# Columns in the first memory piece, held weight transfers and a new order of ScalarE's opening in a two-stack hybrid kernel on one Trainium2 core

## The reference

```python
h = rms_norm(x, norm_pre)
proj = h @ w_in
...
mkv = rms_norm(mem, mem_norm) @ w_mem_kv
mem_k, mem_v = jnp.split(mkv, 2, axis=-1)
y_xa = flat(memory_attention(heads(xa_q), heads(mem_k), heads(mem_v)))
...
up = jnp.einsum('bsnw,nwd->bsnd', ys, w_up)
merged = jnp.sum(jax.nn.sigmoid(gates.reshape(b_, s_, N_BRANCH, D_MODEL)) * up, axis=2)
out = merged @ w_out
return x + rms_norm(out, norm_post)
```

## Time and profile before

| what | before |
|---|---|
| median of 3 runs | 1752.31 us (1752.08 to 1752.43) |
| the profiled execution | 1751.61 us, span 1749.8 us |
| TensorE busy | 1734.2 us, 99% of the span, 9136 matmuls |
| VectorE busy | 1307.9 us, 75% |
| ScalarE busy | 1017.4 us, 58% |
| GpSimd busy | 99.6 us, 6% |
| mean granted TensorE clock | 0.997 of full |
| data moved | 308.70 MB, mean 176 GB/s |
| chain that ended last | TensorE 93%, VectorE 3%, ScalarE 2% |

### The profile page before, as it was taken

How to read it: one execution, slowest core, us unless ns; L and a number is a source line. 1 busy time by engine, 2 the same in 40 slices (tenths; PEclk the granted TensorE clock), 3 DMA queues, 4 the chain that set the end, 5 groups by cost and what they waited for, 6 DMA issues and landing times.

```text
span 1749.8 us, 24255 instructions
## 1 busy us (share of the span) xinstructions
PE 1734.2 (99%) x9136; PEld 1495.1 (85%) x9136; DVE 1307.9 (75%) x1747; ACT 1017.4 (58%) x1406; POOL 99.6 (6%) x154
## 2 busy tenths in 40 slices
PE   8999999999999999999999999999999999999998
PEld 7888888888888888888889988888888988888887
DVE  6787767665877786756669787688778987678775
ACT  5676656454666755644555765755556656555544
POOL 1000000000000000000000000500003360000000
PEclk9999999999999999999999999999999999999999
DMA  9755655566765565565666554456555515356563
GB/s 303 205 156 175 181 159 166 165 187 190 248 183 161 172 181 170 156 181 169 192 194 198 182 192 157 144 182 192 191 186 188 170 37 181 121 168 189 188 189 108
DMA packets 211028, 308.70 MB, mean 176 GB/s; under 512 B 11808, under 2 KB 114848, under 8 KB 210656
## 3 DMA queue, kind: packets, MB, share of 16 engines
q1 hardware_dynamic: 208640, 299.44, 55.5%
q0 software_dynamic: 2128, 7.66, 1.3%
q10 hardware_dynamic: 144, 0.05, 0.0%
HBM read 306.06 MB, written 1.05 MB: 176 GB/s over the span
## 4 chain that ended last, share of the span: by engine, by line
PE 93%; DVE 3%; ACT 2%; issue 1%; DMA 0%; SPq 0%; DVEq 0%; ACTq 0%
PE bank L1701 51%; PE bank L1766 26%; PE bank L1733 3%; PE bank L2168 3%; PE bank L2217 2%; DVE weights_lo L1050 1%; PE bank L1816 1%; PE bank L1830 1%; PE bank L2089 1%; PE bank L2107 1%; PE bank L1799 1%; ACT weights_hi L570 1%; PE bank L1838 0%; DVE arena L1104 0%; DMA weights_raw<-in_w_mem_kv_dram 0%
## 5 line engine op out<-in xcount | busy, mean ns | idle before, releaser
L1050 DVE TENSOR_TENSOR weights_lo<-weights_raw,weights_hi 128x1024 fp32r<-128x1024 f32 x560 | 668.3, 1232 | 222.4 <-ACT weights_hi L570 216.7
L570 ACT ACTIVATE weights_hi<-weights_raw 128x1024 fp32r<-128x1024 f32 x559 | 574.4, 1056 | 395.6 <-DMA weights_raw<-in_w_in_dram 188.0
L1701 PE MATMUL bank<-weights_hi,h_parts 128*128 128x512 f32 x1856 | 567.5, 391 | 0.3 <-DVE h_parts L1482 0.2
L1701 PEld LDWEIGHTS bank<-weights_hi,h_parts 128*128 128x128 f32 x1856 | 348.0, 188 | 73.3 <-DVE h_parts L1482 0.6
L1701 PE MATMUL bank<-weights_lo,h_parts 128*128 128x512 f32 x928 | 347.5, 389 | 0.0
L1766 PE MATMUL bank<-h_parts,weights_hi 128*128 128x512 f32 (+1 forms) x1248 | 302.7, 384 | 0.9 <-DVE arena L1104 0.8
L1701 PE MATMUL bank<-weights_hi,arena_parts 128*128 128x512 f32 x928 | 269.9, 390 | 0.0
L1766 PEld LDWEIGHTS bank<-h_parts,weights_hi 128*128 128x128 f32 x1248 | 219.8, 189 | 40.5 <-DVE arena L1104 1.5
L1701 PEld LDWEIGHTS bank<-weights_lo,h_parts 128*128 128x128 f32 x928 | 174.3, 188 | 35.4
L1701 PEld LDWEIGHTS bank<-weights_hi,arena_parts 128*128 128x128 f32 x928 | 173.6, 188 | 35.4 <-ACT arena L590 0.2
L1766 PEld LDWEIGHTS bank<-h_parts,weights_lo 128*128 128x128 f32 x1248 | 169.4, 190 | 11.1
(11 more groups left out here) (306 smaller groups left out, 1629.4 us busy)
## 6 DMA issues: line engine op xcount, KB each, us to landing
weights_raw<-in_w_in_dram SPq DMA_DIRECT2D x224, 512.0 KB, 3.7
weights_raw<-in_f_w_up_dram SPq DMA_DIRECT2D x96, 512.0 KB, 3.5
weights_raw<-in_f_w_down_dram SPq DMA_DIRECT2D x48, 512.0 KB, 3.6
weights_raw<-in_w_up_dram SPq DMA_DIRECT2D x40, 512.0 KB, 3.6
weights_raw<-in_c_w_pw_dram SPq DMA_DIRECT2D x24, 512.0 KB, 3.6
weights_raw<-in_ab_w_in_dram SPq DMA_DIRECT2D x20, 512.0 KB, 3.7
weights_raw<-in_w_out_dram SPq DMA_DIRECT2D x16, 512.0 KB, 3.8
weights_raw<-in_xa_wk_dram SPq DMA_DIRECT2D x16, 512.0 KB, 3.4
```

The costliest lines, as they stand in the source:

```text
L570: nc.scalar.activation(w_hi[:, q % SPLIT, 0:w], raw[:, n % RAW, 0:w], ACT.Copy).then_inc(hi_done, 1)
L1050: tt(w_lo[:, n % RAW, 0:w], raw[:, n % RAW, 0:w], w_hi[:, q % SPLIT, 0:w].bitcast(F32), ALU.subtract)\
L1701: return mm(bs[t][:, :], sp_[:, 2 * u + kk, t * P:(t + 1) * P], wp[:, kk, :], start=first and u == us[0] and kk == 0 and n == 0, stop=last ...
```

## The change

- The columns are laid in front of the memory's features in one input, and come with piece 0 in one transfer (308 KB); ScalarE's transfer of them and the semaphore cols_in go.
- SyncE waits before several transfers: for piece 0 before piece 2, for the first half of unit 0 before unit 1, for the rest of unit 0 before unit 2, for piece 2 before unit 3, for unit 1 before x and unit 4, for unit 2 before unit 5.
- ScalarE makes features 2 to 5 before unit 1, and features 6 and 7 behind it. VectorE makes the lo of features 2 and 3 before the lo of unit 0, and those of 4 to 7 before unit 1's.
- TensorE runs ten idle calls instead of six.
- sbz comes before mrs, on TensorE, on ScalarE and in the order of the banks, in both layers.

```diff
@@ sbuf @@
-        memT = sb("mem_features", [P, KD, S])
+        first_rows = sb("mem_features", [P, C_MEM + KD * S])
+        cols, memT = first_rows[:, 0:C_MEM], first_rows[:, C_MEM:].rearrange("p (k s) -> p k s", k=KD)
...
-        cols = sb("vector_columns", [P, 104])
@@ ORDER @@
-                              + two("sbv") + pick("mrs", 0) + two("sbz") + (two("mv") if l else [])
+                              + two("sbv") + two("sbz") + pick("mrs", 0) + (two("mv") if l else [])
@@ SyncE @@
                 k0, k1 = MEM_PIECES[i]
-                sp.dma_start(memT[:, k0:k1, :], A["memT"][:, k0:k1, :]).then_inc(memT_in[i], 16)
+                a, b = (C_MEM + k0 * S if i else 0), C_MEM + k1 * S
+                sp.dma_start(first_rows[:, a:b], A["memT"][:, a:b]).then_inc(memT_in[i], 16)
...
                 if n == 1:
+                    sp.wait_ge(memT_in[0], 16)
                     mem_piece(2)
+                    sp.wait_ge(first_in, 16)
+                if n == 2:
+                    sp.wait_ge(raw_full[0], 16)
+                if n == 3:
+                    sp.wait_ge(memT_in[2], 16)
                 if n == 4:
+                    sp.wait_ge(raw_full[1], 16)
                     for t, s in enumerate((x0_in, x1_in)):
                         sp.dma_start(xs[:, t, :], A["x"][0][t * P:(t + 1) * P, :]).then_inc(s, 16)
                     sp.dma_start(cst[:, 0:P], A["constants"][:, 0:P]).then_inc(ident_in, 16)
+                if n == 5:
+                    sp.wait_ge(raw_full[2], 16)
@@ ScalarE @@
-                    act.dma_start(cols[:, :], A["columns"]).then_inc(cols_in, 16)
                     log_exp_table()
                     hi = M_HL["L0"][0]
-                    act.wait_ge(cols_in, 16)
-                    for i, (k0, k1) in enumerate(MEM_PIECES):
-                        up_to(i + 1)
-                        if i == 0:
-                            continue
-                        act.wait_ge(memT_in[i], 16)
-                        for k in range(k0, k1):
-                            link(nc.scalar.activation(hi[:, k, :], memT[:, k, :], ACT.Copy, scale=cols[:, 8 + k:9 + k]), f"m_hi{k}")
+                    up_to(1)
+                    act.wait_ge(memT_in[0], 16)
+                    for k in range(2, KD):
+                        if k in (2, 4):
+                            act.wait_ge(memT_in[k // 2], 16)
+                        if k == 6:
+                            up_to(2)
+                        link(nc.scalar.activation(hi[:, k, :], memT[:, k, :], ACT.Copy, scale=cols[:, 8 + k:9 + k]), f"m_hi{k}")
                     up_to(5)
...
+                for t in range(NT):
+                    copy(tok(3)[:, t, :], "sbz", t, ACT.Silu, f"sbz{t}")
                 b = filled("mrs")
                 link(nc.scalar.activation(junk[:, 0:S], b[:, 0:S], ACT.Copy), ("free", "mrs", 0), "mrs")
-                for t in range(NT):
-                    copy(tok(3)[:, t, :], "sbz", t, ACT.Silu, f"sbz{t}")
@@ VectorE @@
-                    dve.wait_ge(cols_in, 16)
...
-                        up_to(i + 1)
+                        if i:
+                            up_to(i)
@@ TensorE @@
-                    idle(6)
+                    idle(10)
...
                 proj_T("sbv")
+                proj_T("sbz")
                 pe.wait_ge(act_done, SC.at("mem.rstd1"))
...
-                proj_T("sbz")
@@ host layout @@
+C_MEM = 52 * DEPTH
...
-_LAID = ["memT", "mem_2T", "columns", "columns_2", "gm_wsT", "constants", "windows"]
+_LAID = ["memT", "mem_2T", "columns_2", "gm_wsT", "constants", "windows"]
```

More of the change, by code:

```diff
@@ L158, in build @@
         ident_in, const_in, x0_in, x1_in, mem_in = (sem(n) for n in ("ident_in", "const_in", "x0_in", "x1_in", "mem_in"))
-        cols_in, pos_in, bif_in, cols2_in, mem2_in = (sem(n) for n in ("cols_in", "pos_in", "bif_in", "cols2_in", "mem2_in"))
+        pos_in, bif_in, cols2_in, mem2_in = (sem(n) for n in ("pos_in", "bif_in", "cols2_in", "mem2_in"))
         brow_in, win_in, ws_in, out_done = (sem(n) for n in ("brow_in", "win_in", "ws_in", "out_done"))
@@ L234, in build @@
             ORDER[f"L{l}"] = (four("mk") + (two("mv") if l == 0 else []) + four("hT") + four("sbq") + four("sbk") + pick("mlif", 0)
-                              + two("sbv") + pick("mrs", 0) + two("sbz") + (two("mv") if l else []) + four("sbs") + four("mlq") + four("mlk") + four("sbw") + two("mlv")
+                              + two("sbv") + two("sbz") + pick("mrs", 0) + (two("mv") if l else []) + four("sbs") + four("mlq") + four("mlk") + four("sbw") + two("mlv")
                               + pick("mle", 0) + four("mld") + two("sby", "mlo", "mlz") + four("mls") + two("rtq", "rtk") + four("mly")
@@ L500, in _ @@
                     pool.wait_ge(vec_done, VC.at("n_lo3", "L0"))
-                    pool.dma_start(memT[:, :, :], A["mem_2T"]).then_inc(mem2T_in, 16)
+                    pool.dma_start(first_rows[:, C_MEM:], A["mem_2T"]).then_inc(mem2T_in, 16)
                     pool.wait_ge(vec_done, VC.at("res", "L0"))
@@ L2253, in feature_major @@
 def feature_major(np, m):
-    return np.reshape(m.T, (KD, P, S)).transpose(1, 0, 2)
+    return np.reshape(m.T, (KD, P, S)).transpose(1, 0, 2).reshape(P, KD * S)
 def laid_out(np, inputs):
@@ L2267, in laid_out @@
         second += [I["xa_norm_2"][l], I["xa_mem_norm_2"][l], I["f_norm_2"][l], I["f_dw_w_2"][l], I["f_dw_b_2"][l]]
-    got = {"memT": feature_major(np, I["mem"][0]), "mem_2T": feature_major(np, I["mem_2"][0]), "columns": columns(np, first),
+    got = {"memT": np.concatenate([columns(np, first), feature_major(np, I["mem"][0])], 1), "mem_2T": feature_major(np, I["mem_2"][0]),
            "columns_2": columns(np, second), "gm_wsT": np.transpose(I["gm_ws"], (0, 3, 1, 2)),
```

## The result

The change makes the kernel slower. After takes 1773.8 us (median of 4 runs, 1772.86 to 1774.58), before 1752.37 us on the same chip (4 runs, 1752.08 to 1752.5): the ratio is 1.0122, with a 95% interval of 1.0105 to 1.014. Forecast were 1748.7 us and at most 1750.8.

A forecast was written before the change was run, and what follows sets the result against it. TensorE bounds the kernel (busy 1734.2 of 1749.8 us), leaving mainly the opening's stop and half clock. The path's 4.6 us, capped at 3.6 by unit 9's landing, other terms 0, gave 1748.7 us on the median; range 1747.5 to 1750.8.

The forecast's parts named there:

- part 3: Opening transfers: moving the columns into piece 0 removes one ScalarE issue; bounded at 0.15 us either way, taken as 0.
- Rival D: SyncE's queue: each hold empties the rings, unit 9 lands at 37.4; slower, 1754.8 us; chance 0.05.
- Parts 1 and 2: Opening: ScalarE's earlier parts 2 and 3, and four more idle calls, gain TensorE's path 4.6 us.
- The count without a hold: Opening on TensorE: with unit 1 landing at 10.97, the same count ends at 21.45 and gains 3.5 us.
- The four terms: TensorE's opening: stop of 5.66 us and half-clock loss of 1.5, partly paid back by idle calls (1.9) and new waits (1.0).
- the added idle calls cost nothing: Opening on TensorE: real work starts 1.9 us later, but parts 2 and 3 come only at 8.4 and 8.9.
- Part 4: SyncE's queue: waits before later weight transfers let unit 1 land at 9.8, 1.1 us earlier than 10.97.
- two transfers in flight at 1.4 us each nearly cover the 3.5 us of one: SyncE's queue: with two transfers always allowed in flight, the later holds should leave no gap.
- rival B: SyncE's queue: holds bring no landing forward, unit 9 at 32.35 to 32.9; 2.5 to 1.95 us gained; chance 0.20.
- What is late next: First projection on h: unit 9, landing at 31.25, lets the gains start at 33.6; 3.6 us gained, not 4.6.
- rival C: First projection on h: unit 9 lands before 30.3 and does not bind; all 4.6 us gained, 1747.7; chance 0.18.
- Part 5: sbz ahead of mrs: the 0.42 us wait at mrs goes, 0.7 appears at mlq; sum 0, bounds -0.4 and +0.3.

The follow-up runs named there:

- e1: The changed kernel plus 24 unused words per partition behind the features, a shift of 512 bytes instead of 416: 1749.46 us, ratio 0.9982 to before.
- e3: The kernel before with only 104 unused words (416 bytes) between mem_features and weights_raw: 1776.99 us.
- e15: The kernel before with only the new opening order of ScalarE and VectorE and ten idle calls, buffers where they were: 1749.11 us.
- e11: e1 with six idle calls instead of ten: 1749.57 us.
- e9: e1 without any of SyncE's six waits: 1747.02 us in one run.
- e13: The kernel of e9 (e1 without SyncE's six waits), timed more often: 1747.98 us over 9 runs, ratio 0.9975 to before.
- e5: The kernel before with 8 unused words ahead of h_parts, so all buffers from h_parts on move 32 bytes together: 1752.79 us.
- e14: The kernel before with only the columns moved into piece 0, plus 24 unused words: 1752.08 us in one run.
- e8: The kernel before with only 32 unused words (128 bytes) between mem_features and weights_raw: 1769.10 us.
- e4: The kernel before with only 8 unused words (32 bytes) between mem_features and weights_raw: 1770.98 us.

## Why the prediction was wrong

**The step that failed is part 3, the columns in piece 0.** It counted the transfer (52 KB, 0.15 us) and one issue, and took 0. It left out that the columns also move buffers, and held every matmul after 40 us for unchanged. The runs put the price at 24.3 us (after against e1), and at 24.5 in the kernel before (e3). Rival D, the one slower case, looked for it on the queue at 1754.8; no rival held it. The diff showed it: `memT`'s place had grown by `C_MEM` words in the middle of the list of buffers.

About 1 of the 24.3 us may not belong to the matmuls: after and e1 have the same opening, but in their traces the copy of unit 9 starts at 33.66 and 32.36 and the first matmul on h at 36.48 and 35.44. Nothing here explains that difference.

The other steps are judged on e1, which has the change without this.

- **Parts 1 and 2: right.** ScalarE made parts 2 and 3 at 6.89 (predicted 7.4), and the stop of 5.66 us went. The real matmuls begin a little later than the 8.0 counted, at 8.31. TensorE's wait for unit 1's low half was predicted at 0.7 us:

```profile
14.48 1.21 PE L1776 MATMUL bank<-arena_parts,weights_lo 128*128 128x256 f32 x8 [0.69 <-DVE weights_lo L1060]
...
35.44 1.94 PE L1776 MATMUL bank<-h_parts,weights_hi 128*128 128x256 f32 x8
```

 The count without a hold gave 3.5 us of gain; e15, which is that case, has 3.4. (The four terms that the prediction names for this path, 5.66, 1.5, 1.9 and 1.0, give 4.3 us and not 4.6; the 4.6 comes from its count of times.) The statement that the added idle calls cost nothing is borne out by e11. But they also gained nothing.
- **Part 4, the holds: wrong.** Unit 1 was to land at 9.8 and did at 10.49; the kernel without holds has it at 9.60 (e9) and 10.59 (e13). The end of mk moved with it, to about 21.1 instead of 20.35. That "two transfers in flight at 1.4 us each nearly cover the 3.5 us of one" was the mistaken term: at 305 instead of 372 GB/s they don't. Unit 4 came at 19.53, only 0.8 us before TensorE was to begin on it by the count of part 2 (20.35), and its hi and lo copies take 1.06 and 1.23 us. This was rival B, whose numbers fit e1 (unit 9 at 32.34, gains at 34.82), and a little of D; the holds cost about 1.5 us. That e1's 1749.46 is still so near the forecast 1748.7 is in part luck: see below.
- **What is late next: wrong for e1, right in the one trace of after.** Unit 9's landing was to cap the gain, with a wait of about 1 us near 33 in front of the gains. In after it was so: the copy of unit 9 started at 33.66 and TensorE waited 1.25 us for h_parts. In e1 ScalarE's timeline reads

```profile
32.36 1.06 ACT L581 ACTIVATE weights_hi<-weights_raw 128x1024 fp32r<-128x1024 f32 x1 [0.43 <-DMA weights_raw<-in_w_in_dram]
33.33 1.21 ACT L701 ACTIVATE arena<-bank 128x512 f32<-128x512 f32 x2
34.82 2.00 ACT L662 ACTIVATE h_parts<-bank,mem_features 128x256 fp32r<-128x256 f32 x4 [0.28 <-PE bank L1840]
```

 The gains waited for TensorE, not for the unit. TensorE itself was late: of the 4.6 us counted for it 2.4 were left. Of the rest 0.8 were lost by the end of mk, and it had waited at 21.93 (0.65 us) and again at 27.89 (0.19 us) for low halves of the late units. Where nothing held the queue (e13) unit 9 landed at 30.42, and TensorE reached h at 34.10 without a wait for h_parts. That is close to rival C (unit 9 before 30.3, 1747.7 us), but with the holds gone. The issues of units 8 and 9 wait for TensorE's slots, so they come earlier when TensorE does; the prediction took their landing as fixed.
- **Part 5, sbz ahead of mrs: right**, in total and in place: 0.66 us at the mlq matmul (predicted 0.7), sum 0.

Forecast for all but the placement was 3.6 us of gain (1748.7). e1 has 3.0, with 2.4 of it at the first matmul on h. The profiled executions differ by 2.1 us only (1751.61 and 1749.53); the rest is that before's profiled execution lies 0.9 below its median of 1752.5, so the nearness of 3.0 to 3.6 is no proof of the sum.

## What to carry to other kernels

A change that adds, drops or resizes one buffer moves all that are laid behind it, and a matmul's time can depend on how its two operands stand to each other. Before costing such a diff, list what moves against what, and compare the time from start to start of the main matmul groups in both kernels: a few nanoseconds each, in one group and not in its neighbour, is the sign. Here a filler that made the added distance 512 bytes, a multiple of 256, separated this from all else in one run. And when a chain is shortened, landings of transfers that wait for that chain's slots move along. Holding transfers back to "help" the first ones brought those nothing here, and left the queue emptier (305 for 372 GB/s).

## What the hardware showed that was not expected

- **The distance of TensorE's two operands.** A matmul of 512 columns takes 227.0 ns from start to start with weights and h_parts 0, 256 or 512 bytes from their old distance, and 232.4 to 234.3 at 32, 128, 416 and 448. For `proj_H` at 512 columns it is 229.9 and 232.6 to 233.2, but 229.3 at 448, where those of 256 columns with the lo half even fall from 119.1 to 116.3. So the old place isn't the best for every form. Moving both operands together by 32 bytes changes nothing (e5). Not tried: other distances, above all between 448 and 512.
- **Two transfers in flight did not fill the engines.** With SyncE allowing about two 512 KB transfers at once the rate from 6 to 16 us was 305 GB/s, without the limit 372.
- **The first landings may gain from one transfer less on a second queue; this is not settled.** Without ScalarE's own transfer of the columns (128 rows of 416 bytes) and without holds the copy of unit 1 started at 9.68 (e9), 10.40 (e14) and 10.67 (e13); with it, in before, e3 to e8 and e15, at 10.55 (e4) to 11.17 (e5). The two groups overlap, one execution each.
- **The same 20 idle records** took 7.47 us in e1, 6.74 in e9 and 5.99 in e13: the time at which the full clock is granted differs between executions, from 4.08 us (e13) to 7.07 (e1). A difference of a microsecond in the opening, seen in one execution, says nothing.
